# A hybrid decoder layer: three weight pieces issued earlier, and gate products split into single-pass matmuls

## The chip, the cores and the metric

The kernel runs on one core of a Trainium2 chip. The metric is the device time of one execution in microseconds (us). Before the change the median of three runs is 1207.89 us (1207.12 to 1209.24).

## The reference, cut to what matters

One layer over 256 prompt tokens and 8 x 8 sample tokens (320 in all), model width 1024. The change touches only the dense stage ahead of the mixture of experts:

```
proj = x @ w_in + b_in                       # 1024 -> 7 x 1024
xa, ga, b_gate, c_gate, v_sc, m_a, m_b = split(proj, 7)
xa_c = causal_dwconv(xa, width 4) + conv_a_b
r = sigmoid(blockdiag(wa) @ xa_c + ba)       # 16 heads of 64 x 64
i = sigmoid(blockdiag(wx) @ xa_c + bx)
a = exp(-8 r softplus(-lambda)); b = sqrt(1 - a^2) * i * xa_c
h = scan(a, b);  y_a = h * gelu(ga)
y_b = b_gate * causal_dwconv(c_gate * v_sc, width 3)
mixed = (sigmoid(m_a) * y_a + sigmoid(m_b) * y_b) @ w_out
```

Behind it stand a layer norm, a router, 32 experts of which each token takes 4, and a second layer norm. All inputs and outputs are float32.

## The kernel before, in words

The dense stage holds everything with channels on partitions. It runs in eight rounds c = 0..7, one for each group of 128 channels. A round takes seven pieces of `w_in`, each 1024 x 128, in the order XA, CG, V, GA, BG, MA, MB (j = 0..6); piece q = 7c + j is 512 KB.

A float32 product is made of three single-pass products in the type float32r. Each piece lands in one of four slots of `raw` (`load_piece`, L308 to L312). ScalarE rounds it to `w_hi` (L453, `split_high`); VectorE subtracts to get `w_lo` (L992, `split_low`, called `ahead(j)` in the rounds). TensorE then runs 8 x 3 matmuls over 320 tokens (L658): hi by hi, hi by lo, lo by hi. A piece may be loaded only when the split of the piece four before it is done (semaphore `lo_ok`), and TensorE starts a piece only when its own split is.

After the seventh piece of a round, TensorE multiplies the convolved `xc` by the two gate matrices of this round (L668). These are plain float32 matmuls, each recorded as two passes. The matrices are copied beforehand from `wab`, where all gate weights lie as 128 x 128 blocks, to `wcur` (L1064). TensorE waits for `wcur_ok`, `xc_ok` and for the banks of the gates to be free.

ScalarE takes each piece's result out of PSUM (L488 to L498), then the gate results through tanh (L502, L504), a second tanh (L507) and a square root (L509); only then does it reach the next `split_high`.

VectorE's order in a round is written out by hand: copy of the gate weights, `ahead(4)`, the first convolution (L1070 to L1077), `ahead(5)`, the second convolution (L1084 to L1092), `ahead(6)` to `ahead(9)`, in rounds 1 to 3 a `bias_low` for the expert biases (L1043), the merge of the gates MA and MB (from L1098), the wait for ScalarE's tanh, `ahead(10)`, a reciprocal (L1112), the scan (L1121) and the block of `mixT` (L1125).

SyncE issues nearly all loads in one queue, in program order: x, pieces 0 and 1, parameter rows, states, pieces 2 and 3, four loads of gate weights into `wab` (L352, 256 B rows; they need the memset of `wab`), eight loads of bias rows (L358, L360), then pieces 4 to 55, between which eight halves of the first experts' weights are issued (L331), one of them after `bias_ok`. At the end come the four loads of `w_out` (L378), the last of which waits for the last piece's products. VectorE waits for all gate weights once, ahead of round 0 (L1045).

After the rounds TensorE multiplies `mixT` by `w_out` (L678). The expert stage streams 192 units of 2 MB through ten slots; each load waits until TensorE has used the slot.

Of the kernel before, what the change touches and what calls it, by code (L numbers as in the profile page):

```python
# [13 lines left out]
P = 128  # L14
D = 1024
# [3 lines left out]
T = SEQ + NS  # L19
TILES = [(0, P), (P, P), (2 * P, NS)]  # L20
IN_W = 7 * D
NP = 7 * KC
# [16 lines left out]
XA, GA, BG, CG, V, MA, MB = range(7)  # L39
# [5 lines left out]
ALU = mybir.AluOpType  # L45
ACT = mybir.ActivationFunctionType
AX_X = mybir.AxisListType.X
F32 = mybir.dt.float32
F32R = mybir.dt.float32r
I32 = mybir.dt.int32  # L50
U32 = mybir.dt.uint32
ds = bass.ds
# [25 lines left out]
def hybrid_layer(nc, x_prompt, x_sample, state_h, state_conv, state_sc, w_in, b_in, conv_a_w,  # L78
# [5 lines left out]
    with ctx:  # L84
# [3 lines left out]
        def sem(name):  # L88
            return ctx.enter_context(nc.semaphore(name))
# [5 lines left out]
        slot = 4 * WIDE  # L95
        XT, X1 = SLOTS * slot, SLOTS * slot + 12 * D
# [4 lines left out]
        def place(name, shape, offset, dt=F32):  # L101
            return nc.alloc_sbuf_tensor_at(name, shape, dt, offset=base + offset)
# [36 lines left out]
        y_acc = x_tok  # L139
        wab = x1[:, 0:2, :].rearrange("p a (c n) -> p a c n", c=KC)  # L140
        st_rows = x1[:, 2, :]

# [34 lines left out]
        PS = ctx.enter_context(nc.psum_tensor("PS", [P, 8, HALF], F32))  # L179


        tiles = place("tiles", [P, 12 * T + 2 * P], 5 * slot)
        bgt, cgt, vt, gel, tma, tmb, xc, tr, ti, rr, aa, sq = (tiles[:, i * T:(i + 1) * T] for i in range(12))
        wcur = tiles[:, 12 * T:12 * T + 2 * P].rearrange("p (a n) -> p a n", a=2)
        hh = vt
        uc = cgt
        xa_p, xa_s = xa_pad[:, 0:259], xa_pad[:, 259:347].rearrange("p (b s) -> p b s", b=DB)
# [63 lines left out]
        gates_done, gates_taken = sem("gates_done"), sem("gates_taken")  # L251
        wcur_ok = sem("wcur_ok")
        prm_ok = sem("prm_ok")
        xa_free, cv_free, xc_ok, block_ok = sem("xa_free"), sem("cv_free"), sem("xc_ok"), sem("block_ok")
        t_ok, sq_ok = sem("t_ok"), sem("sq_ok")
        xlo_ok = sem("xlo_ok")
        wout_done, shifted = sem("wout_done"), sem("shifted")
# [49 lines left out]
        def _(sp):  # L307
# [36 lines left out]
            sp.dma_start(st_rows[0:8, :], state_h[0]).then_inc(st_in, 16)  # L344
            sp.dma_start(st_rows[8:32, :], state_conv[0].rearrange("b j d -> (b j) d")).then_inc(st_in, 16)
            sp.dma_start(st_rows[32:48, :], state_sc[0].rearrange("b j d -> (b j) d")).then_inc(st_in, 16)
            for q in range(2, 4):
                load_piece(q)
            sp.wait_ge(zero_ok, 1)
            for a, w in enumerate((lru_wa, lru_wx)):  # L350
                for j in range(2):
                    sp.dma_start(wab[64 * j:64 * j + 64, a, :, 64 * j:64 * j + 64],  # L352
                                 w[0].rearrange("(c j) i o -> j i c o", j=2)[j]).then_inc(wab_in, 16)

            for a in range(2):
                for h in range(2):
                    rows = slice(64 * a + 32 * h, 64 * a + 32 * h + NE)
                    sp.dma_start(bias_raw[rows, 0:2 * HALF].rearrange("p (b n) -> p b n", b=2),  # L358
                                 b_gu[0].rearrange("e (b a n) -> a e b n", a=2, b=2)[a]).then_inc(bias_in, 16)
                    sp.dma_start(bias_raw[rows, 2 * HALF:3 * HALF],  # L360
                                 b_down[0, :, a * HALF:(a + 1) * HALF]).then_inc(bias_in, 16)

            for q in range(4, NP):
                load_piece(q)
                if q % 4 == 3 and q < 7 + 4 * KC:
                    k = (q - 7) // 4
                    if k == 6:
                        sp.wait_ge(bias_ok, 1)
                    load_half(k // 2, k % 2)
# [49 lines left out]
            for q, (t, _) in enumerate(LAST_SUMS):  # L419
                t0, n = TILES[t]  # L420
# [26 lines left out]
        def _(act):  # L447
# [24 lines left out]
            for q in range(NP):  # L472
                c, j = q // 7, q % 7
                m = ORDER[j]
                bias = prm[:, BIN + m * KC + c:BIN + m * KC + c + 1]
                if 0 < q < NP - AHEAD:
                    split_high(q + AHEAD)
                if q == 5:
                    act.wait_ge(prm_ok, 3)
                if q == 8:  # L480
                    act.wait_ge(bias_in, 128)
                    act.activation(bias4[:, :, :].rearrange("p b n -> p (b n)"), bias_raw, ACT.Copy)\
                       .then_inc(bias_hi, 1)
                act.wait_ge(proj_done, q + 1)
                ps = PS[:, j % 6, 0:T]
                if m == XA:
                    act.wait_ge(xa_free, c + 1)
                    act.activation(xa_p[:, 3:259], pr(ps), ACT.Identity, bias=bias)  # L488
                    act.activation(xa_s[:, :, 3:11], sm(ps), ACT.Identity, bias=bias).then_inc(proj_taken, 1)
                elif m in (CG, V, BG):  # L490
                    if m == CG:
                        act.wait_ge(block_ok, c + 1)
                    act.activation({CG: cgt, V: vt, BG: bgt}[m], ps, ACT.Identity, bias=bias).then_inc(proj_taken, 1)
                elif m == GA:
                    act.activation(gel, ps, ACT.Gelu_apprx_tanh, bias=bias).then_inc(proj_taken, 1)
                else:
                    dst, o = (tma, c) if m == MA else (tmb, KC + c)
                    act.activation(dst, ps, ACT.Tanh, bias=bhalf[:, o:o + 1], scale=0.5).then_inc(proj_taken, 1)  # L498
                if j == 6:

                    act.wait_ge(gates_done, 2 * c + 2)
                    act.activation(ti, PS[:, 7, 0:T], ACT.Tanh, bias=ghalf[:, KC + c:KC + c + 1], scale=0.5)\  # L502
                       .then_inc(gates_taken, 1)
                    act.activation(tr, PS[:, 6, 0:T], ACT.Tanh, bias=ghalf[:, c:c + 1], scale=0.5)\  # L504
                       .then_inc(gates_taken, 1)
                    act.wait_ge(gates_taken, 2 * c + 4)
                    act.activation(tr, tr, ACT.Tanh, bias=sp2[:, c:c + 1], scale=sp2[:, c:c + 1]).then_inc(t_ok, 1)  # L507
                    act.wait_ge(t_ok, c + 1)
                    act.activation(sq, tr, ACT.Sqrt).then_inc(sq_ok, 1)  # L509
# [14 lines left out]
            for q, t in enumerate(T_ORDER):  # L524
                n = TILES[t][1]
# [76 lines left out]
            for q, (t, _) in enumerate(LAST_SUMS):  # L602
                n = TILES[t][1]
# [11 lines left out]
        def _(pe):  # L615
            mm = pe.matmul
# [15 lines left out]
            for k in range(KC):  # L632
                for t, (t0, n) in enumerate(TILES):
                    last = pe.transpose(PS[:, k, t0:t0 + n], x_tok[0:n, t, k * P:(k + 1) * P], ident[0:n, 0:n])
# [14 lines left out]
            for q in range(NP):  # L649
                c, j = q // 7, q % 7  # L650
                pe.wait_ge(lo_ok, q + 1)
                if q > 0:
                    pe.wait_ge(proj_taken, 7 * c + {0: 8, 6: 9}.get(j, j + 2))
                for k in range(KC):
                    if q == 0:
                        pe.wait_ge(xlo_ok, k + 1)
                    for n, (w, x) in enumerate(((w_hi, x_hi), (w_hi, x_lo), (w_lo, x_hi))):
                        last = mm(PS[:, j % 6, 0:T], w[:, q % RING, k, :], x[:, k, :],  # L658
                                  start=(k == 0 and n == 0), stop=(k == KC - 1 and n == 2))
                last.then_inc(proj_done, 1)  # L660
                if q == 0:
                    turn_rows()
                if j == 6:
                    pe.wait_ge(wcur_ok, c + 1)
                    pe.wait_ge(xc_ok, c + 1)
                    pe.wait_ge(gates_taken, 2 * c + 2)
                    for a in range(2):
                        mm(PS[:, 6 + a, 0:T], wcur[:, a, :], xc, start=True, stop=True).then_inc(gates_done, 1)  # L668

# [17 lines left out]
            for a in range(2):  # L689
                last = project(2, a, [KC - 1])  # L690
# [37 lines left out]
            for k in range(KC):  # L728
                last = pe.transpose(PS[0:54, 6 + k // 4, (k % 4) * P:(k % 4 + 1) * P], so[:, k, :], ident[:, :])
# [11 lines left out]
               start=False, stop=False)  # L741
# [241 lines left out]
        def _(dve):  # L983
# [53 lines left out]
            def bias_low(c, a):  # L1037

                if c == 1:
                    dve.wait_ge(bias_hi, 1)  # L1040
                rows = slice(64 * a + 32, 64 * a + 64)
                part = bias4[rows, c - 1, :]
                return dve.tensor_tensor(part, bias_raw[rows, (c - 1) * HALF:c * HALF], part.bitcast(F32), ALU.subtract)  # L1043

            dve.wait_ge(wab_in, 64)  # L1045
            for c in range(KC):
                def ahead(j):
                    if 7 * c + j < NP:
                        split_low(7 * c + j)

                def taken(j):
                    dve.wait_ge(proj_taken, c * 7 + (KC + j))
# [7 lines left out]
                def by_seq(ap, j):  # L1060
                    return ap.rearrange("p (b j) -> p b j", j=j)


                dve.tensor_copy(wcur[:, :, :], wab[:, :, ds(c, 1), :].rearrange("p a c n -> p (a c) n"))\  # L1064
                   .then_inc(wcur_ok, 1)

                link(dve.tensor_copy(xa_s[:, :, 0:3], by_seq(state(8, 24), 3)))
                ahead(4)
                taken(1)
                dve.tensor_scalar(pr(xc), xa_p[:, 0:SEQ], par(CAW, c), par(CAB, c), ALU.mult, ALU.add)  # L1070
                link(dve.tensor_scalar(sm(xc), xa_s[:, :, 0:DS], par(CAW, c), par(CAB, c), ALU.mult, ALU.add))
# [23 lines left out]
                    ahead(j)  # L1095
                if 1 <= c <= 3:
                    bias_low(c, 0)
                taken(7)  # L1098
                link(stt(tmb, tmb, 1.0, bgt, ALU.add, ALU.mult))
                link(dve.tensor_tensor(tmb, tmb, uc, ALU.mult))  # L1100
# [311 lines left out]
```

## Time and profile before

| | |
|---|---|
| profiled execution | 1207.79 us, span 1206.0 us |
| median of three runs | 1207.89 us |
| TensorE matmul busy | 1152.4 us (96%) |
| VectorE busy | 514.4 us (43%) |
| ScalarE busy | 255.7 us (21%) |
| mean granted TensorE clock | 0.992 |
| dense stage, to the end of the seventh piece of round 7 | 0 to 224.1 us |

Times in the rows count from the first instruction. PE is TensorE, PEld its weight loads, DVE VectorE, ACT ScalarE, SPq the queue of SyncE that issues DMAs. In a list in order of time a row gives start, duration, engine and line, operation, output and input, count, and in brackets the idle time of the engine ahead of it and what ended that. Neighbouring instructions of one line are merged (x24). Matmuls overlap, so their pace is read from the distance of their starts.

### The profile page before, as it was taken

The page shows a single profiled execution, that of the slowest core. Times are in us where ns is not written, and L with a number is a line of the kernel's source. Part 1 is how long each engine was busy: PE and PEld are TensorE (multiplying, and loading weights), DVE is VectorE, ACT ScalarE, POOL GpSimd, SP SyncE. Part 2 cuts the span into 40 slices and gives each one's busy share as a digit, 9 for nine tenths or more (in the row PEclk, how much of TensorE's full clock was granted, in tenths as well). Part 3 has the DMA queues.
Part 4 walks back from the last instruction along what each step waited for, and adds up shares of the span by engine and source line. Part 5 has one row for each costly group of instructions (what it writes and reads, how often), then busy time and mean ns, then how long its engine had stood idle before and what let it go on. Part 6 is the DMA issues. An engine that isn't in the chain of part 4 may idle for free.

```text
span 1206.0 us, 13920 instructions
## 1 busy us (share of the span) xinstructions
PE 1152.4 (96%) x5682; PEld 556.0 (46%) x5682; DVE 514.4 (43%) x982; ACT 255.7 (21%) x398; POOL 3.3 (0%) x13
## 2 busy tenths in 40 slices
PE   8999999999999999999999989999999999999994
PEld 8999999654333333333333323333333333333331
DVE  5888888563422322233323322232222222222236
ACT  4655655311111111111111111111111111111112
POOL 1000000000000000000000000000000000000000
PEclk9999999999999999999999999999999999999998
DMA  9766844748999999999999999999999999999994
GB/s 234 227 210 195 244 131 138 300 177 332 400 429 427 427 429 427 427 427 429 426 427 429 427 427 428 428 427 426 429 427 428 428 426 429 428 426 428 427 425 165
DMA packets 93404, 443.77 MB, mean 368 GB/s; under 512 B 7848, under 2 KB 65336, under 8 KB 67998
## 3 DMA queue, kind: packets, MB, share of 16 engines
q1 hardware_dynamic: 93246, 442.67, 90.7%
q8 instruction: 45, 0.74, 0.3%
q10 hardware_dynamic: 96, 0.22, 0.0%
q14 instruction: 17, 0.14, 0.0%
HBM read 441.34 MB, written 1.53 MB: 367 GB/s over the span
## 4 chain that ended last, share of the span: by engine, by line
PE 58%; DMA 28%; DVE 7%; issue 2%; ACT 2%; SPq 2%; DVEq 0%; ACTq 0%
DMA ring<-in_w_gu 24%; PE PS L846 20%; PE PS L886 13%; PE PS L658 7%; PE PS L754 6%; DMA ring<-in_w_down 3%; PE PS L776 3%; PE PS L678 2%; DVE w_lo L992 2%; DVE tiles L1035 1%; PE PS L762 1%; PE PS L769 1%; DVE tiles L1112 1%; PE PS L926 1%; PE PS L809 1%
## 5 line engine op out<-in xcount | busy, mean ns | idle before, releaser
L846 PE MATMUL PS<-ring,mid 128*64 128x512 f32 x1920 | 423.0, 594 | 24.4 <-DMA ring<-in_w_gu 23.7
L846 PEld LDWEIGHTS PS<-ring,mid 128*64 128x64 f32 x1920 | 135.4, 137 | 305.1 <-issue 254.8
L886 PE MATMUL PS<-ring,mid 128*64 128x512 f32 x960 | 213.1, 595 | 0.0
L1301 DVE TENSOR_SCALAR PS<-PS 128x512 f32<-128x512 f32 x30 | 21.0, 700 | 358.1 <-PE PS L846 358.1
L658 PE MATMUL PS<-x_hi,w_hi 128*128 128x320 f32 x448 | 141.5, 316 | 2.6 <-DVE w_lo L992 2.0
L658 PE MATMUL PS<-x_hi,w_lo 128*128 128x320 f32 x448 | 139.1, 311 | 0.0
L658 PE MATMUL PS<-x_lo,w_hi 128*128 128x320 f32 x448 | 139.1, 310 | 0.0
L1283 DVE TENSOR_TENSOR ys<-PS,ys 64x512 fp32r<-64x512 f32 x64 | 44.1, 688 | 193.9 <-ACT ys L572 185.6
L886 PEld LDWEIGHTS PS<-ring,mid 128*64 128x64 f32 x960 | 66.1, 137 | 130.1 <-issue 130.0
L1035 DVE SCALAR_TENSOR_TENSOR x_tok<-PS,gate,x_tok 128x1024 f32<-128x1024 f32 (+1 forms) x93 | 115.1, 1275 | 20.8 <-PE PS L776 20.8
L563 ACT ACTIVATE mid<-PS 128x512 f32<-128x512 f32 x30 | 17.9, 598 | 423.8 <-DVE PS L1301 423.8
L754 PE MATMUL PS<-x,onehot 128*64 128x512 f32 (+1 forms) x396 | 98.8, 617 | 2.9 <-DVE esel L1200 2.9
L658 PEld LDWEIGHTS PS<-x_hi,w_hi 128*128 128x128 f32 x448 | 84.7, 189 | 5.6 <-DVE w_lo L992 4.7
L658 PEld LDWEIGHTS PS<-x_lo,w_hi 128*128 128x128 f32 x448 | 84.7, 189 | 0.3
L658 PEld LDWEIGHTS PS<-x_hi,w_lo 128*128 128x128 f32 x448 | 84.7, 189 | 0.0
L572 ACT ACTIVATE ys<-PS 64x512 fp32r<-64x512 f32 x60 | 35.6, 593 | 209.1 <-PE PS L886 208.4
L992 DVE TENSOR_TENSOR w_lo<-raw,w_hi 128x1024 fp32r<-128x1024 f32 x56 | 67.0, 1223 | 19.9 <-ACT w_hi L453 19.4
L776 PE MATMUL PS<-ys,onehotT 128*128 128x512 f32 (+1 forms) x186 | 64.7, 431 | 0.0
L453 ACT ACTIVATE w_hi<-raw 128x1024 fp32r<-128x1024 f32 x56 | 59.1, 1055 | 21.2 <-DMA raw<-in_w_in 21.2
L754 PEld LDWEIGHTS PS<-x,onehot 128*64 128x64 f32 (+1 forms) x396 | 22.8, 136 | 55.9 <-issue 52.1
L776 PEld LDWEIGHTS PS<-ys,onehotT 128*128 128x128 f32 (+1 forms) x186 | 25.5, 176 | 25.4 <-issue 25.2
L678 PE MATMUL PS<-ring,mixT 128*128 128x512 f32 (+1 forms) x96 | 35.3, 597 | 1.4 <-DMA ring<-in_w_out 1.4
(232 smaller groups left out, 726.3 us busy)
## 6 DMA issues: line engine op xcount, KB each, us to landing
ring<-in_w_gu SPq DMA_DIRECT2D x124, 2048.0 KB, 39.8
ring<-in_w_down SPq DMA_DIRECT2D x62, 2048.0 KB, 38.8
raw<-in_w_in SPq DMA_DIRECT2D x56, 512.0 KB, 5.5
ring<-in_w_gu SPq DMA_DIRECT2D x8, 1024.0 KB, 8.2
ring<-in_w_out SPq DMA_DIRECT2D x4, 1024.0 KB, 6.0
ring<-in_w_down SPq DMA_DIRECT2D x4, 1024.0 KB, 41.4
x_tok<-in_x_prompt SPq DMA_DIRECT2D x1, 1024.0 KB, 5.4
out<-x SPq DMA_DIRECT2D x2, 512.0 KB, 2.7
```

What stands on the lines that cost most here:

```text
L453: act.activation(w_hi[:, q % RING], raw[:, q % RING], ACT.Copy).then_inc(hi_ok, 1)
L572: act.activation(y_rows(a, 0), PS[64 * a:64 * a + 64, XB, :], ACT.Copy).then_inc(yhi_ok, 1)
L658: last = mm(PS[:, j % 6, 0:T], w[:, q % RING, k, :], x[:, k, :], start=(k == 0 and n == 0), stop=(k == KC - 1 and n == 2))
L678: last = mm(out, mixT[:, k, t0:t0 + n], slot_out[:, k // 2, k % 2, a * HALF:(a + 1) * HALF], start=(k == 0), stop=(k == KC - 1))
L754: last = mm(PS[64 * a:64 * a + 64, XB, :], onehot[0:n, t, :], x1[0:n, t, a * HALF:(a + 1) * HALF], start=(t == 0), stop=(t == 2))
L776: last = mm(PS[0:n, bank + a, :], onehotT[:, par, t0:t0 + n], ys[:, a, :], start=True, stop=True)
L846: last = mm(PS[64 * a:64 * a + 64, b, :], xgT[:, 2 * (u % 2) + j, u // 2, :], w[:, o:o + HALF], start=False, stop=(u == 3 and j == 1))
L886: last = mm(PS[64 * a:64 * a + 64, XB, :], hT[:, j, u, :], w[:, j * D + a * HALF:j * D + (a + 1) * HALF], start=(u == 0 and j == 0), stop= ...
L992: dve.tensor_tensor(w_lo[:, q % RING], raw[:, q % RING], w_hi[:, q % RING].bitcast(F32), ALU.subtract).then_inc(lo_ok, 1)
L1035: return dve.scalar_tensor_tensor(out=out, in0=in0, scalar=scalar, in1=in1, op0=op0, op1=op1)
L1283: last = dve.tensor_tensor(y_rows(a, 1), PS[64 * a:64 * a + 64, bank, :], y_rows(a, 0).bitcast(F32), ALU.subtract)
L1301: dve.tensor_scalar(gm, gm, LIMIT, None, ALU.min).then_inc(gm_ok, 1)
```

## The change

On the loads: piece 4 is issued right behind pieces 2 and 3, ahead of the gate weights; pieces 5 and 6 are issued between the gate weights and the bias rows; the rest follows from piece 7.

On the gate products: ScalarE rounds `xc` to `xc_hi` after it has taken the BG piece; VectorE copies the gate weights to `gate_hi` (in place of the copy to `wcur`), subtracts to get `gate_lo` after `ahead(4)`, and subtracts to get `xc_lo` after `ahead(9)` and `bias_low`. TensorE runs three single-pass matmuls for each gate and waits for `xc_lo` (semaphore `xclo_ok`) in place of `xc_ok`. The new tiles lie in the space of the state rows, which have been read by then.

```
@@ sync
-            for q in range(2, 4):
+            for q in range(2, 5):
                 load_piece(q)
             sp.wait_ge(zero_ok, 1)
...
+            for q in range(5, 7):
+                load_piece(q)
             for a in range(2):
                 for h in range(2):
...
-            for q in range(4, NP):
+            for q in range(7, NP):
@@ scalar
                     act.activation({CG: cgt, V: vt, BG: bgt}[m], ps, ACT.Identity, bias=bias).then_inc(proj_taken, 1)
+                    if m == BG:
+                        act.wait_ge(xc_ok, c + 1)
+                        act.activation(xc_hi[:, :], xc, ACT.Copy).then_inc(xchi_ok, 1)
@@ tensor
                     pe.wait_ge(wcur_ok, c + 1)
-                    pe.wait_ge(xc_ok, c + 1)
+                    pe.wait_ge(xclo_ok, c + 1)
                     pe.wait_ge(gates_taken, 2 * c + 2)
                     for a in range(2):
-                        mm(PS[:, 6 + a, 0:T], wcur[:, a, :], xc, start=True, stop=True).then_inc(gates_done, 1)
+                        for n, (w, x) in enumerate(((gate_hi, xc_hi), (gate_lo, xc_hi), (gate_hi, xc_lo))):
+                            last = mm(PS[:, 6 + a, 0:T], w[:, a, :], x[:, :], start=(n == 0), stop=(n == 2))
+                        last.then_inc(gates_done, 1)
@@ vector
-                dve.tensor_copy(wcur[:, :, :], wab[:, :, ds(c, 1), :].rearrange("p a c n -> p (a c) n"))\
-                   .then_inc(wcur_ok, 1)
-
+                gates_w = wab[:, :, ds(c, 1), :].rearrange("p a c n -> p (a c) n")
+                dve.tensor_copy(gate_hi[:, :, :], gates_w)
                 link(dve.tensor_copy(xa_s[:, :, 0:3], by_seq(state(8, 24), 3)))
                 ahead(4)
+                dve.tensor_tensor(gate_lo[:, :, :], gates_w, gate_hi[:, :, :].bitcast(F32), ALU.subtract)\
+                   .then_inc(wcur_ok, 1)
                 taken(1)
...
                 if 1 <= c <= 3:
                     bias_low(c, 0)
+                dve.wait_ge(xchi_ok, c + 1)
+                dve.tensor_tensor(xc_lo[:, :], xc, xc_hi[:, :].bitcast(F32), ALU.subtract).then_inc(xclo_ok, 1)
                 taken(7)
```

## Rows read from the trace of the kernel before

**Rows 1.** Chain of waits in order of time: start, duration, engine and line.
```profile
63.96 3.79 PE PS L658 x24
...
220.30 3.80 PE PS L658 x24
...
224.12 7.58 DMA ring<-in_w_out
```
**Rows 2.** Weight loads' waits, 0 to 260 us: total, times, longest.
```profile
PEld PS L658 <- DVE w_lo L992: 4.7, 8, 2.3
```
**Rows 3.** TensorE in order of time, round 0.
```profile
26.95 0.31 PE L658 MATMUL PS<-x_hi,w_lo 128*128 128x320 f32 x1
29.30 0.42 PE L658 MATMUL PS<-x_hi,w_hi 128*128 128x320 f32 x1 [2.04 <-DVE w_lo L992]
...
30.39 0.47 PE L658 MATMUL PS<-x_hi,w_hi 128*128 128x320 f32 x1
30.66 0.47 PE L658 MATMUL PS<-x_lo,w_hi 128*128 128x320 f32 x1
...
41.35 0.31 PE L658 MATMUL PS<-x_hi,w_lo 128*128 128x320 f32 x1
```
**Rows 4.** TensorE in order of time, end of round 5, and at w_out.
```profile
168.12 0.41 PE L658 MATMUL PS<-x_hi,w_hi 128*128 128x320 f32 x1
...
171.59 0.31 PE L658 MATMUL PS<-x_hi,w_lo 128*128 128x320 f32 x1
171.73 1.24 PE L668 MATMUL PS<-tiles 128*128 128x320 f32 x4
...
231.83 4.71 PE L678 MATMUL PS<-ring,mixT 128*64 128x512 f32 x12 [1.36 <-DMA ring<-in_w_out]
```
**Rows 5.** SyncE's queue in order of time.
```profile
11.14 2.72 SPq L352 DMA_DIRECT2D x<-in_lru_wa  x2
...
21.92 1.05 SPq L312 DMA_DIRECT2D raw<-in_w_in  x2
```
**Rows 6.** Line 352 alone: time from issue to landing of its loads.
```profile
DMA to landing us min/median/max: 5.1/6.2/6.9
```
**Rows 7.** ScalarE in order of time.
```profile
26.86 1.06 ACT L453 ACTIVATE w_hi<-raw 128x1024 fp32r<-128x1024 f32 x1 [7.71 <-DMA raw<-in_w_in]
...
168.05 0.53 ACT L498 ACTIVATE tiles<-PS,dsm 128x320 f32<-128x320 f32 x1 [2.04 <-PE PS L658]
```
**Rows 8.** VectorE in order of time, start and round 0.
```profile
10.62 1.22 DVE L992 TENSOR_TENSOR w_lo<-raw,w_hi 128x1024 fp32r<-128x1024 f32 x1 [0.45 <-ACT w_hi L453]
...
22.70 0.28 DVE L1064 COPY tiles<-x 128x256 f32<-128x256 f32 x1
...
28.02 1.23 DVE L992 TENSOR_TENSOR w_lo<-raw,w_hi 128x1024 fp32r<-128x1024 f32 x1 [4.95 <-ACT w_hi L453]
...
32.08 1.22 DVE L992 TENSOR_TENSOR w_lo<-raw,w_hi 128x1024 fp32r<-128x1024 f32 x1
...
36.09 3.50 DVE L992 TENSOR_TENSOR w_lo<-raw,w_hi 128x1024 fp32r<-128x1024 f32 x3
```
**Rows 9.** VectorE in order of time, rounds 2, 4 and 5.
```profile
93.38 0.68 DVE L1043 TENSOR_TENSOR bias<-bias_raw,bias 32x512 fp32r<-32x512 f32 x1
...
144.49 1.23 DVE L992 TENSOR_TENSOR w_lo<-raw,w_hi 128x1024 fp32r<-128x1024 f32 x1 [0.20 <-ACT w_hi L453]
...
163.98 0.42 DVE L1084 TENSOR_TENSOR dsm<-tiles 128x256 f32<-128x256 f32 x1
164.31 0.23 DVE L1085 TENSOR_TENSOR dsm<-tiles 128x64 f32<-128x64 f32 x1
...
166.84 4.63 DVE L992 TENSOR_TENSOR w_lo<-raw,w_hi 128x1024 fp32r<-128x1024 f32 x4
```
**Rows 10.** Stretches: busy us and count by engine, granted clock, DMA share, GB/s.
```profile
30.00:32.00 2.00, 2.00 (x11) 2.00 (x10) 1.93 (x8) 1.72 (x3) 0.00 (x0) 0.53 1.10 385
...
224.00:262.00 38.00, 36.64 (x105) 14.84 (x104) 21.76 (x44) 4.89 (x9) 0.00 (x0) 1.00 0.59 242
```

More of the change, by code:

```diff
@@ L141, in hybrid_layer @@
         st_rows = x1[:, 2, :]
+        xc_hi = place("xc_hi", [P, T], X1 + 8 * D, F32R)
+        xc_lo = place("xc_lo", [P, T], X1 + 8 * D + 4 * T, F32R)
+        gate_lo = place("gate_lo", [P, 2, P], X1 + 8 * D + 8 * T, F32R)
         x_hi = place("x_hi", [P, KC, T], 6 * slot, F32R)
@@ L179, in hybrid_layer @@
         PS = ctx.enter_context(nc.psum_tensor("PS", [P, 8, HALF], F32))
-        tiles = place("tiles", [P, 12 * T + 2 * P], 5 * slot)
+        tiles = place("tiles", [P, 12 * T], 5 * slot)
         bgt, cgt, vt, gel, tma, tmb, xc, tr, ti, rr, aa, sq = (tiles[:, i * T:(i + 1) * T] for i in range(12))
-        wcur = tiles[:, 12 * T:12 * T + 2 * P].rearrange("p (a n) -> p a n", a=2)
+        gate_hi = place("gate_hi", [P, 2, P], 5 * slot + 48 * T, F32R)
         hh = vt
@@ L254, in hybrid_layer @@
         xa_free, cv_free, xc_ok, block_ok = sem("xa_free"), sem("cv_free"), sem("xc_ok"), sem("block_ok")
+        xchi_ok, xclo_ok = sem("xchi_ok"), sem("xclo_ok")
         t_ok, sq_ok = sem("t_ok"), sem("sq_ok")
```

## The prediction

> **What bounds the kernel now.** Read the chain of waits in order of time first, then what TensorE waited for, then the single instructions around the places the chain names. The dense stage is eight rounds c = 0..7 of seven projection pieces (piece 7c + j, j = 0..6, 24 matmuls each); call S(c) the start of the seventh piece (j = 6) of round c. In the chain [rows 1] the reader is to see three things. The seventh piece of every round from 1 to 7 stands in it as a step of its own (first 63.96, last 220.30, seven of them, some 26.05 us apart). It is entered from the VectorE split `w_lo`: TensorE's weight loads waited eight times for L992, 4.7 us in all, 2.3 of it once [rows 2], so about 0.35 us in each of the seven other rounds. And the stage ends through the last w_out load, issued when the last piece is done (224.12, landing 7.58 us later), not through the last gate products. So a round is a loop: seventh piece, gate products (L668), ScalarE (tanh, square root), VectorE (reciprocal, scan, next convolution), split of the next seventh piece. VectorE closes it and TensorE has only a third of a microsecond to spare. Everything behind hangs on S(7), because the first expert loads are gated by the last piece, the last block, the projection and x1: I carry a shift of S(7) one to one to the end.
>
> The first wait is another thing. Piece 4 is issued at 21.92 [rows 5], behind four loads of gate weights and eight of bias rows; its high part starts at 26.86 after ScalarE stood 7.71 us [rows 7]; TensorE stops after 26.95 and starts again at 29.30 [rows 3]. Then the stream runs at a start every 0.267 us (30.39 to 30.66) and not 0.147 (171.59 to 171.73 in [rows 4]), with a granted clock of 0.53 in 30 to 32 us [rows 10], the 1.2 GHz level for nearly all of that stretch. S(0) is 41.35 - 23 x 0.147 = 37.97.
>
> **Part 1, the loads.** Piece 4 needs the split of piece 0, done at 10.62 + 1.22 = 11.84 [rows 8], so SP issues it at about 11.9 instead of 21.92; pieces 5 and 6 need splits 1 and 2, done at the latest when TensorE starts piece 2 (27.10 - 48 x 0.147 = 20.0), and follow the gate weights: SP spent 21.92 - 11.14 = 10.8 us on twelve loads [rows 5], so it is at piece 5 some 4 to 5 us after 12.4. At the 4.9 us that piece 4 took (21.92 to 26.86), or half as much again, all three land before their use. The gate weights move from 11.14 to about 12.4, 1.3 us later, and have 0.5 MB more ahead of them. They took 5.1 to 6.9 us to land [rows 6], the last issued near 15. VectorE comes to them at 22.70 [rows 8]; the last of them now lands at about 22 to 23.7, so VectorE stands up to 1 us. Is that hidden? From there it needs, by its old spacing, 0.4 us to split 4, then 32.08 - 28.02 = 4.06 plus a new subtraction of 0.33 to split 5, and 36.09 - 32.08 = 4.01 to split 6, plus 1.22 [rows 8]: 10.0 us. TensorE, with no stop, comes to piece 6 at 26.95 + 0.147 + 48 x 0.147 = 34.15. So the weights may land as late as 24.1 at no cost. I take S(0) = 34.15: **-3.8 us** (2.2 of stop, 1.6 of slow stream). Bias rows and pieces 7 to 9 come 2.6 us later or earlier against the round but are used only from S(0) + 1 on; if piece 9 lands late it costs up to 0.5. Ends: -3.8 and -2.5.
>
> **Part 2, VectorE's two subtractions.** `gate_hi` replaces a copy of the same 128x256 (0.28, [rows 8]): nothing. `gate_lo` is one more 128x256 subtraction of two SBUF tensors, between the split j = 4 and the convolution, where VectorE is on the chain in all rounds. The nearest row is L1084, 128x256 of two tensors: next instruction 164.31 - 163.98 = 0.33 later, itself 0.42 long [rows 9]. Below: 0.20, as a copy; above: 0.42. I take 0.33. It lies in the seven intervals S(c) to S(c+1): **+2.3 us**.
>
> `xc_lo` (128x320; rows of that size take 0.49, as L1043 with 512 elements takes 0.68 [rows 9] and L1084 with 256 takes 0.42) stands behind the splits j = 6..9, and now the gate products wait for it. Queued behind them on TensorE is all of the next round. VectorE's order decides:
> Rounds 5 and 6: four splits from 166.84, spaced (4.63 - 1.22)/3 = 1.137 [rows 9], so `xc_lo` runs 171.39 to 171.88 and TensorE sees it at 171.93 (0.05 as from split to piece: 166.84 + 1.22 to 168.12). Before, the products began at 171.73 [rows 4].
> Rounds 1 to 3: `bias_low` stands between, 93.38 [rows 9] + 0.68 - 0.09 overlap, so `xc_lo` ends at 94.46, seen 94.51, which is S + 4.51; before S + 3.61.
> Round 4: its last split starts only at 144.49 [rows 9]: seen at 146.17, S + 4.14.
> Round 0: the split of piece 9 ends near S + 2.8, `xc_lo` before S + 3.5: no wait. Round 7 has no splits left and is off the path.
>
> **Part 3, the products.** Four passes, 171.73 to + 1.24 [rows 4], end at S + 4.85. Six single passes at 0.147: unhindered they end at 3.61 + 5 x 0.147 + 0.31 = S + 4.65, **-0.20** (round 0). After a wait the first is 0.41 long [rows 4], so they end 0.41 + 0.735 = 1.15 after it: rounds 5 and 6 S + 4.96, **+0.11 each**; rounds 1 to 3 S + 5.66, some **+0.83 each** (round 1's bias row starts a tenth later); round 4 S + 5.29, **+0.43**. ScalarE's next step waits for both products, so these are the loop's. Bounds of a pass: 0.147 and 0.267. The other new instruction, ScalarE's `xc_hi` (about 0.5), comes ahead of a 2.04 us idle [rows 7] and its split is needed 2 us later: nothing; uncovered it would be 0.5 a round.
>
> **Sum.** -3.8 + 2.3 - 0.2 + 3 x 0.83 + 0.43 + 2 x 0.11 = +1.4 us. Against the profiled execution, 1207.79 (span 1206.0), that is 1209.2; the median of the runs, 1207.89, stands 0.1 above it: **1209.3 us**. TensorE loses the gain of the start again in three rounds.
>
> Two rules weighed. The row says that a VectorE instruction starts 0.08 before the one ahead of it ends (1.22 long, 1.137 apart, [rows 9]). The Trainium skill, "VectorE: DVE Perf Modes", section "Terms", says of the flush after every operation: "next op can't issue until 8-slice pipe empties". By that the two subtractions would cost about 0.09 more each in seven rounds, +1.3 us; the trace disagrees for the splits, so it is only rival 3. On the loads: the gate weights landed in 5.1 to 6.9 us for 128 KB each [rows 6], against 4.9 for a 512 KB piece [rows 5, 7]. The Trainium skill, "DMA: Bandwidth & Descriptors", section "Specifications", asks for at least 512 B per transfer for line rate, and these move rows of 64 floats, 256 B. It speaks against putting anything ahead of them; by the row the cost is the 1 us of standing counted above, hidden.
>
> **Rivals.**
> 1. TensorE is the bound and VectorE follows. For it: it is 96% busy over the span, and waits only 0.35 us a round [rows 2]. Then only the start counts and the products give 0.2 in seven rounds: -5.2, 1202.6. Half of it, the wait for `xc_lo` costing nothing but `gate_lo` counting: -3.8 - 1.4 + 2.3 = -2.9, 1205.0. Against: the wait for the split recurs in all seven rounds, so VectorE is late already.
> 2. The clock falls again in the new stops. Place: ahead of the products in rounds 1 to 3, about 1 us each. Price: the 1.6 us paid after the stop of 2.2, three times: +4.8, 1214.1, slower. It decides if such a stop is enough. Against: a stop of 1.36 at 231.83 left the granted clock at 1.00 [rows 4, 10].
> 3. VectorE's added work costs full lengths: +2.7, 1210.6, slower by a little more than can be told.
> 4. The start gives less: gate weights land after 24.1, each microsecond later costs one, or piece 4 waits for an instruction ahead of it in ScalarE's or VectorE's order, so that the reordering does not do what it says: 2 us lost, 1211.3.
>
> **How the numbers follow.** Forecast 0.52, rival 1 0.15, rival 2 0.08, rival 3 0.15, rival 4 0.10. A measurement of this kernel can tell about 0.2%, 2.4 us, from no change: 1205.5 to 1210.3. Of the forecast's share 0.42 lies within, 0.07 above, 0.03 below; rival 1 is faster; rivals 3 and 4 are half within and half above; rival 2 above. Faster 0.18, same 0.54, slower 0.28. The likeliest case alone spans 1207.5 to 1211 (its bounds: `gate_lo` 0.20 to 0.42, the start -2.5); the range takes in half of rival 1 and most of rival 4: 1205 to 1212.5.
>
> **What would show it.** After: no stop of TensorE near 27 us and no 0.267 spacing at 30 (part 1); S(0) near 34.1; VectorE's copy of the gate weights at 22.7 to 23.7. Intervals S(c) to S(c+1) of 26.1 in round 0, 27.2 in 1 to 3, 26.8 in 4, 26.5 in 5 and 6. The products start on a wait for VectorE's subtraction, 1 us in rounds 1 to 3, 0.2 in 5 and 6; the waits for `w_lo` at the seventh piece stay and grow to 0.5. S(7) near 221.7. The prediction is wrong if intervals stay at 26.05 or less, if the seventh piece no longer waits, or if the granted clock dips in rounds 1 to 3.

## The result, and the profile after

The changed kernel is slower: median 1214.12 us (1212.82 to 1217.17, four runs) against 1207.51 (1206.55 to 1209.24, four runs), a ratio of 1.0062 on record (95% interval 1.0048 to 1.0076; the two medians alone give 1.0055, and the ratios below are likewise those on record). The forecast was 1209.3, at most 1212.5. The profiled execution is the longest of the four (1217.17, span 1214.3; the shortest span is 1211.0), so of the rows below those behind the dense stage show its upper end.

Chain of waits after, in order of time (start, duration, engine and line; L667 are the projection matmuls, L678 the gate products, L689 the product with w_out). It answers to [rows 1] and [rows 3].

```profile
16.54 21.32 PE PS L667 x144
37.86 2.63 issue
40.48 1.78 PE PS L678 x6
42.26 25.51 PE PS L667 x168
...
91.09 3.78 PE PS L667 x24
94.88 0.89 issue
95.76 1.13 PE PS L678 x6
...
225.29 3.80 PE PS L667 x24
...
229.11 8.83 DMA ring<-in_w_out
...
238.07 31.60 PE PS L689 x72
```

The stop near 27 us is gone: 144 projection matmuls run without a gap to 37.86, so S(0), reckoned from the start of the last matmul (37.55, below) as in the prediction, is 37.55 - 23 x 0.147 = 34.17 (forecast 34.15, before 37.97). Then comes a step that the chain before did not have: 2.63 us of "issue" ahead of the first gate products. "Issue" hides its releaser here; TensorE's own rows show the place, and what the stop did to the stream behind it (the bracket is the idle time before a row):

```profile
37.55 0.31 PE L667 MATMUL PS<-x_hi,w_lo 128*128 128x320 f32 x1
40.48 0.44 PE L678 MATMUL PS<-xc_hi,gate_hi 128*128 128x320 f32 x1 [2.63 <-issue]
40.73 0.47 PE L678 MATMUL PS<-xc_hi,gate_lo 128*128 128x320 f32 x1
...
44.15 0.31 PE L667 MATMUL PS<-x_hi,w_lo 128*128 128x320 f32 x1
```

Starts are 0.25 to 0.27 us apart up to 43.9 and 0.147 from 44.15. Busy time by stretch (columns as in [rows 10], the granted clock third from the end) gives the clock beside it:

```profile
40.00:42.00 2.00, 1.51 (x6) 1.55 (x7) 1.77 (x4) 0.00 (x0) 0.00 (x0) 0.67 1.03 395
42.00:44.00 2.00, 2.00 (x9) 2.00 (x9) 0.00 (x0) 1.65 (x4) 0.00 (x0) 0.50 1.03 324
...
94.00:120.00 26.00, 24.89 (x167) 24.25 (x167) 22.54 (x51) 15.26 (x22) 0.00 (x0) 1.00 0.61 174
238.00:240.00 2.00, 1.93 (x5) 0.73 (x6) 0.38 (x1) 0.00 (x0) 0.00 (x0) 0.66 0.94 389
```

The 1.2 GHz stretch has moved from 30 us [rows 10] to 42 us; it has not gone. It does not come in round 2 (94 to 120), where the stop is 0.89. It comes again at 238, behind a stop of 2.81 us for w_out that was 1.36 before [rows 4].

Why do the products wait at 37.86? VectorE's rows, then ScalarE's, then SP's queue:

```profile
22.43 0.29 DVE L1076 CAST gate_hi<-x 128x256 fp32r<-128x256 f32 x1
...
37.02 1.22 DVE L1003 TENSOR_TENSOR w_lo<-raw,w_hi 128x1024 fp32r<-128x1024 f32 x1 [3.13 <-ACT w_hi L459]
...
38.76 1.22 DVE L1003 TENSOR_TENSOR w_lo<-raw,w_hi 128x1024 fp32r<-128x1024 f32 x1 [0.51 <-ACT w_hi L459]
...
39.90 0.48 DVE L1111 TENSOR_TENSOR xc_lo<-tiles,xc_hi 128x320 fp32r<-128x320 f32 x1
```
```profile
31.57 1.06 ACT L459 ACTIVATE w_hi<-raw 128x1024 fp32r<-128x1024 f32 x1 [1.89 <-DMA raw<-in_w_in]
...
35.93 1.06 ACT L459 ACTIVATE w_hi<-raw 128x1024 fp32r<-128x1024 f32 x1 [2.52 <-DMA raw<-in_w_in]
...
37.67 1.06 ACT L459 ACTIVATE w_hi<-raw 128x1024 fp32r<-128x1024 f32 x1 [0.27 <-DMA raw<-in_w_in]
```
```profile
20.39 1.88 SPq L364 DMA_DIRECT2D bias_raw<-in_b_gu  x1
...
27.02 0.42 SPq L316 DMA_DIRECT2D raw<-in_w_in  x1
27.49 0.58 SPq L335 DMA_DIRECT2D ring<-in_w_gu  x1
28.11 7.67 SPq L316 DMA_DIRECT2D raw<-in_w_in  x4
```

Read from the bottom: SP spends 20.39 to 27.0 on the eight bias rows, issues piece 7 at 27.02, then a 1 MB half unit of the expert weights, then pieces 8 and 9. Their high parts wait for the DMA three times, by 1.89, 2.52 and 0.27 us, and the splits on VectorE follow at 32.67, 37.02 and 38.76. `xc_lo` stands behind all of them in VectorE's program and is done at 40.38, 0.10 before TensorE goes on. Before, the gate products read the convolution's output directly, and nothing in them waited for a split.

### The profile page after: what moved, and what is told of

Read it like the earlier page. It is cut to its first block, busy times and chain, and to the rows that moved or that the text cites. A ratio compares the mean times of both kernels' runs of the same rounds, so it can differ in the third digit from the quotient of the medians.

```text
span 1214.3 us, 13976 instructions
## 1 busy us (share of the span) xinstructions
PE 1156.5 (95%) x5698; PEld 558.5 (46%) x5698; DVE 520.3 (43%) x998; ACT 257.6 (21%) x406; POOL 3.3 (0%) x13
## 4 chain that ended last, share of the span: by engine, by line
PE 62%; DMA 25%; DVE 9%; issue 2%; ACT 2%; DVEq 0%; POOL 0%; ACTq 0%; POOLq 0%
PE PS L857 22%; DMA ring<-in_w_gu 21%; PE PS L897 14%; PE PS L765 6%; PE PS L667 6%; DMA ring<-in_w_down 3%; PE PS L787 3%; PE PS L689 3%; DVE w_lo L1003 2%; DVE tiles L1046 2%; PE PS L773 1%; DVE tiles L1126 1%; PE PS L780 1%; PE PS L820 1%; PE PS L937 1%
## 5 line engine op out<-in xcount | busy, mean ns | idle before, releaser
L857 PE MATMUL PS<-ring,mid 128*64 128x512 f32 x1920 | 423.2, 594 | 23.0 <-DMA ring<-in_w_gu 22.7
L667 PE MATMUL PS<-x_hi,w_hi 128*128 128x320 f32 x448 | 140.6, 314 | 1.3 <-DVE w_lo L1003 1.3
L667 PE MATMUL PS<-x_lo,w_hi 128*128 128x320 f32 x448 | 139.0, 310 | 0.0
L667 PE MATMUL PS<-x_hi,w_lo 128*128 128x320 f32 x448 | 138.9, 310 | 0.0
L667 PEld LDWEIGHTS PS<-x_hi,w_hi 128*128 128x128 f32 x448 | 84.6, 189 | 4.1 <-DVE w_lo L1003 3.9
L667 PEld LDWEIGHTS PS<-x_lo,w_hi 128*128 128x128 f32 x448 | 84.6, 189 | 0.0
L667 PEld LDWEIGHTS PS<-x_hi,w_lo 128*128 128x128 f32 x448 | 84.5, 189 | 0.0
L689 PE MATMUL PS<-ring,mixT 128*128 128x512 f32 (+1 forms) x96 | 37.0, 619 | 2.8 <-DMA ring<-in_w_out 2.8
```

Source lines behind the costliest of these rows:

```text
L689: last = mm(out, mixT[:, k, t0:t0 + n], slot_out[:, k // 2, k % 2, a * HALF:(a + 1) * HALF], start=(k == 0), stop=(k == KC - 1))
L857: last = mm(PS[64 * a:64 * a + 64, b, :], xgT[:, 2 * (u % 2) + j, u // 2, :], w[:, o:o + HALF], start=False, stop=(u == 3 and j == 1))
```

## The experiments

Each kernel was timed in five rounds beside the kernel before on the same chip. e1 to e12 are their short names. First the two parts by themselves.

**The loads alone** (e1), on the kernel before:

```diff
-            for q in range(2, 4):
+            for q in range(2, 5):
                 load_piece(q)
...
+            for q in range(5, 7):
+                load_piece(q)
...
-            for q in range(4, NP):
+            for q in range(7, NP):
```

> The new order of loads with the gate products as before. Theory A (the loads' gain of 3.8 us is real and is thrown away only because the gate products now wait behind the splits of pieces 8 and 9, whose loads land late): the gate products of round 0 start at S(0) + 3.6, near 37.7, the seventh piece of round 1 near 60.2, and all of the 3.8 us stay: 1203.8. Theory B (the late pieces 8 and 9 hold round 0 whatever the gate products wait for, through VectorE's order): S(1) near 63.5 and 1207, within 0.5 of before.

1203.77 against 1206.39: ratio 0.9980 (0.9971 to 0.9988), 2.6 us faster, and S(7) at 217.74, 2.6 earlier. The loads do what the prediction said, for less: S(0) is 34.73, and S(1) 61.54, 2.4 earlier than before. The same late pieces 7 to 9 are in this trace (waits of 1.34, 2.89 and 0.23 us), but the products do not depend on splits; the lateness only makes ScalarE late to free a bank of PSUM (the memory that holds the matmuls' results), for which the first piece of round 1 waits:

```profile
40.35 0.38 PE L660 MATMUL PS<-x_hi,w_hi 128*128 128x320 f32 x1 [0.87 <-ACT tiles L500]
```

**The split products alone** (e2): the changed kernel with SP's order of before (the diff above, reversed).

> The split gate products with the old order of loads. Theory A: round 0 costs +0.1, rounds 1 to 6 together +4.8 as in the changed kernel (27.2 us a round in 1 to 3, 26.5 in 4 to 6), and what follows the w_out load 0 to 3 us: 1212.7 to 1215, as slow as the whole change. Theory B (the loads are what makes the change slow, by the stop of 2.9 us ahead of the first gate products and the fallen clock behind it): 1209 or less.

1214.56: ratio 1.0058 (1.0045 to 1.0071), as slow as the whole change. S(0) is 36.92 and S(7) 224.83, so seven rounds take 187.9 instead of 182.3 [rows 1, 3], +5.6, where parts 2 and 3 together forecast +5.2. The 0.4 is round 0: its products do not stop, but they start at S(0) + 3.85, where the forecast had S(0) + 3.61. So the split is sized about right, and the 2.6 us that the loads give alone are worth nothing under it.

This profile shows one thing more. It has the kernel before's order of loads, and its first stop is 1.10 us and not 2.04, with the granted clock at 1.00 from 26 to 38 us. e11 below, whose dense stage is the kernel before's, has 0.83 there, the clock at 1.00, and S(0) at 36.59 and S(7) at 218.90. So the 2.04 us and the slow stream behind it are those of one profiled execution; how often they come is not known. Against e11 the moved loads bring S(0) forward by 2.4, not 3.8.

**Who holds the products up in round 0?** On the changed kernel, the half units two pieces later (e4); then that and the eight bias rows behind piece 9 as well (e5):

```diff
-            for a in range(2):            # the bias rows' loop
...
             for q in range(7, NP):
                 load_piece(q)
+                if q == 9:
+                    for a in range(2):    # the bias rows' loop, e5 alone
...
-                if q % 4 == 3 and q < 7 + 4 * KC:
-                    k = (q - 7) // 4
+                if q % 4 == 1 and 9 <= q < 9 + 4 * KC:
+                    k = (q - 9) // 4
```

> The whole change, with each half of an expert unit issued two pieces later, so that the first stands behind piece 9 and not between pieces 7 and 8. Theory A1 (that 1 MB load ahead of piece 8 makes pieces 8 and 9 late): they land 3 us earlier, the stop ahead of round 0's gate products goes from 2.9 us to under 0.5, the clock doesn't fall there, S(1) near 60.4: 3.8 us less than the change, 1210.3. Rival A2 (the bias rows ahead of piece 7 do it): the stop stays over 2 us and the time within 1 us of the change, 1214.

1211.35, ratio 1.0040 (1.0027 to 1.0053). The stop shrank by 1 us only: piece 7 is still behind the bias rows, issued at 27.84, and its high part begins at 33.54. (The changed kernel's own stop differs between profiles: it is 2.63 in the profile above, 1.92 in e8 and 2.75 in e9, whose dense stage is the same.)

```profile
37.97 1.62 issue
39.59 1.13 PE PS L678 x6
...
62.26 3.78 PE PS L667 x24
```

> The whole change, with the bias rows issued behind piece 9 (they stood ahead of piece 7) and each half unit two pieces later. e4 left a stop of 1.6 us, as piece 7 was still late and held ScalarE's splits. Theory A (the failed step of the prediction is only the late pieces 7 to 9): pieces 7 to 9 are split in time, the stop ahead of round 0's products is under 0.4 us, S(1) near 60.4, the other intervals stay at 27.2 and 26.5, S(7) near 221.7, 1.4 us behind the kernel before; with the unsteady part behind the w_out load +1.4 to +3.5. Rival A3 (something else in round 0 holds the products, ScalarE's order or the parameters): the stop stays over 1.3 us and the time 5 us above before.

1209.78, ratio 1.0028 (1.0019 to 1.0036): 2.8 us over the kernel before, with the split in it. The stop is gone and S(1) is where the prediction had it (60.25):

```profile
37.82 0.95 PE PS L678 x6
...
60.43 3.78 PE PS L667 x24
...
118.75 1.75 issue
...
222.66 3.79 PE PS L667 x24
...
226.47 6.29 DMA ring<-in_w_out
```

S(7) is 222.66 (forecast 221.7). The missing 0.9 is the stop at 118.75, 1.75 where rounds 1 and 2 have 0.89. ScalarE and VectorE ahead of it, one row each:

```profile
116.87 1.06 ACT L459 ACTIVATE w_hi<-raw 128x1024 fp32r<-128x1024 f32 x1 [1.55 <-DMA raw<-in_w_in]
```
```profile
117.96 1.23 DVE L1003 TENSOR_TENSOR w_lo<-raw,w_hi 128x1024 fp32r<-128x1024 f32 x1 [0.78 <-ACT w_hi L459]
```

The last split waited for its high part, and that for its piece. A half unit is issued 4 us ahead of that piece (106.95 and 110.95). e4 has the same half unit there; the piece's high part waits 0.68 in it, and the stop stays at 0.88. So the order of the loads makes this piece late in both, but what made it later in e5 is not shown.

**The wait for `xc_lo` and `gate_lo`.** On the changed kernel both subtractions are moved up, right behind the split of the seventh piece (j = 6) and ahead of the three splits j = 7 to 9, where they wait for ScalarE's `xc_hi` (e3); and `xc_lo` alone (e7):

```diff
-                dve.tensor_tensor(gate_lo[:, :, :], gates_w, gate_hi[:, :, :].bitcast(F32), ALU.subtract)...
...
+                    if j == 6:
+                        dve.wait_ge(xchi_ok, c + 1)
+                        dve.tensor_tensor(xc_lo[:, :], xc, xc_hi[:, :].bitcast(F32), ALU.subtract)...
+                        dve.tensor_tensor(gate_lo[:, :, :], gates_w, gate_hi[:, :, :].bitcast(F32), ALU.subtract)...
...
-                dve.wait_ge(xchi_ok, c + 1)
-                dve.tensor_tensor(xc_lo[:, :], xc, xc_hi[:, :].bitcast(F32), ALU.subtract)...
```

> The whole change, with both of VectorE's subtractions right behind the split of the seventh piece (ahead of splits j = 7 to 9) instead of ahead of the convolution and behind the splits. Theory A (they cost by their place: gate_lo lies on VectorE's way to the seventh piece, xc_lo on the gate products' way): no stop ahead of the products in any round, intervals of 25.85 us, S(7) 5.2 earlier than before: 1202.4. Rival C (VectorE's time is what counts, wherever it is spent): intervals stay at 26.5 and above, 1207 or more.

1204.71, ratio 0.9985 (0.9976 to 0.9994). VectorE no longer closes the rounds; TensorE runs through them at 25.7 to 25.9 us a round:

```profile
39.72 24.87 PE PS L667 x168
64.59 0.88 PE PS L678 x6
...
91.29 24.93 PE PS L667 x168
116.22 0.88 PE PS L678 x6
...
215.90 3.80 PE PS L667 x24
```

The 6 products take 0.88 in the chain, the 4 of the kernel before took 1.09 there: 0.2 a round is all that the split gives, once nothing waits. It shows rival 1's case, TensorE the bound, as one that this placement makes and the changed kernel's did not.

> The whole change with only the xc_lo subtraction moved ahead of the splits j = 7 to 9; gate_lo stays ahead of the convolution. If gate_lo costs its 0.33 us on VectorE's way to the seventh piece, the intervals are 26.05 - 0.20 + 0.33 = 26.2 us in all rounds, against 25.8 to 25.9 in e3: S(7) 2.0 later than e3, near 218, and xc_lo's place is then worth the rest, 7 us, of which 2.9 are round 0's stop and the clock behind it. If gate_lo is hidden, the intervals are those of e3.

1206.60, ratio 1.0004 (0.9993 to 1.0014); S(7) 217.79, rounds of 26.10 to 26.22. With `gate_lo` on VectorE's chain VectorE closes the rounds again. The 26.05 of before, less 0.2 for the products, plus the 0.33 of part 2 makes 26.18 (an estimate): `gate_lo` costs what was forecast, and S(7) is 1.9 later than in e3.

**The late loads and both placements mended** (e6: e5's loads, e3's placement):

> As e5, and both subtractions behind the split of the seventh piece as in e3. Theory A: no stop anywhere in the dense stage, TensorE bound by its own 25.8 us a round; against e3 the 1.0 us that TensorE stood ahead of round 1 (for ScalarE, which was held by pieces 8 and 9) goes too: S(7) near 214.9, 5.4 us before the kernel before, time 3.3 to 5.4 us less. Rival: no better than e3, whose time was 0.15% below before.

1202.24, ratio 0.9967 (0.9953 to 0.9980): 4.7 us under its kernel before of 1206.95, the lowest ratio of the study, though its interval still touches e3's. S(1) is 60.64, S(7) 215.70, and the last w_out load lands in 6.17 us. Expected was 214.9 for S(7): once the subtractions are moved, the later bias rows and half units bring it only 0.2 forward against e3.

**The clock in round 0's stop.** On the changed kernel, ten matmuls whose results are overwritten, ahead of the wait, in round 0 alone (e12):

```diff
                     pe.wait_ge(wcur_ok, c + 1)
-                    pe.wait_ge(xclo_ok, c + 1)
                     pe.wait_ge(gates_taken, 2 * c + 2)
+                    if c == 0:
+                        for _ in range(10):
+                            mm(PS[:, 6, 0:T], x_hi[:, 0, 0:P], x_hi[:, 0, :], start=True, stop=True)
+                    pe.wait_ge(xclo_ok, c + 1)
```

> The changed kernel with ten more 128x320 matmuls on TensorE in round 0 alone, whose results are overwritten, between the last projection piece of the round and its wait for xc_lo. Theory C: of the 4.0 us by which S(1) came later than forecast (64.25 against 60.25), 2.6 are the stop before the gate products and about 1.4 the clock that falls in it (products 1.78 instead of 1.13 us, the 168 matmuls behind 25.51 instead of 24.7). The filler takes 1.5 us of the stop, which shrinks to about 1.2 with the products starting where they did (near 40.5); the granted clock stays at 1.00, the 168 matmuls take 24.7 and S(1) comes near 62.9. Round 1 is then closed by TensorE; S(7) near 223.9 and the time 1.4 below the changed kernel, near 1212.6. Rival V: the stop alone makes the loss, since VectorE's split closes the round whatever TensorE's clock does: S(1) stays within 0.3 of 64.25 and the time at 1214.

1213.70 against 1207.49, ratio 1.0054 (1.0041 to 1.0068). TensorE's rows, the chain and the stretches in this kernel (L681 are its products):

```profile
37.44 1.63 PE L677 MATMUL PS<-x_hi 128*128 128x320 f32 x10
41.04 0.42 PE L681 MATMUL PS<-xc_hi,gate_hi 128*128 128x320 f32 x1 [1.97 <-DVE xc_lo L1114]
```
```profile
41.04 1.16 PE PS L681 x6
...
225.49 3.80 PE PS L667 x24
```
```profile
42.00:44.00 2.00, 2.00 (x16) 2.00 (x15) 0.49 (x2) 1.73 (x4) 0.00 (x0) 1.00 0.98 347
```

Here TensorE's wait has its name: `xc_lo`. The clock stays at 1.00, the full 2.4 GHz level. The products start 0.56 later (piece 9 came 0.6 later in this execution) and take 1.16 instead of 1.78, so they end at 42.20 against 42.26, and S(7) is 225.49 against 225.29: nothing gained. Both theories had a part wrong. S(1) came 0.35 earlier (63.74 against 64.09; the 64.25 of the expectation is a quarter of a microsecond too late), but round 1 gave it back. The end of the products sets the round: from it to the next seventh piece's start lie 21.5 us on ScalarE and VectorE (42.20 to 63.74 here, 40.72 to 62.26 in e4). In the changed kernel it is 21.8, as TensorE comes 0.3 late, but from the end of these products to the start of round 1's lie 26.23 us there and 26.26 here: TensorE's slow stream up to 44.1 is hidden. What is left of the fallen clock is the 0.6 us by which it stretches the products themselves; that these would be gained in a run whose piece 9 is no later was not shown. Nor is the stream always hidden: in e8 the clock falls only behind the products (end 41.24), and round 1's products start 26.74 us later, 0.5 more.

**Behind S(7).** Two attempts on the stop before w_out. A filler of six matmuls there (e8):

```diff
                 pe.wait_ge(block_ok, k + 2)
+                if k == 6:
+                    pe.wait_ge(bias_ok, 1)
+                    keep_warm(6, 5)
                 pe.wait_ge(wout_in[k // 2], 16)
```

> The whole change, with six matmuls of 128x512 (1.3 us, results unused) ahead of the wait for the last w_out load. Theory D (the stop of 2.8 us there lets the clock fall, which costs 1.65 us in the w_out product, and whether it falls makes the runs of this kernel spread over 4 us): the granted clock stays at 1.00 behind the stop, the w_out product takes 29.95 us and not 31.6, the runs lose their upper half; median 1 to 1.5 us below the change, whose ratio to before was 1.0062. Rival: the clock has no part in it, the ratio stays at 1.0062 or more.

1213.99, ratio 1.0063 (1.0050 to 1.0076). In the profile the 72 matmuls take 29.95 and the clock does not fall there, as that theory wanted, but the median stays where the changed kernel's is. Its profiled execution was again an end of the spread (1212.59, the shortest of six), so it does not decide it.

Then the last w_out load by itself, the expert units behind it issued only when it has landed, on the changed kernel (e9), on e6's version (e10) and on the kernel before (e11):

```diff
             sp.wait_ge(proj_done, NP)
+            sp.wait_ge(wout_in[3], 16)
             load_unit(4)
```

> The changed kernel, with one wait added on SP: the first of the two 2 MB expert units that SP issues 0.4 to 1.0 us behind the last w_out load now waits until that load has landed. Theory T: what the changed kernel loses behind S(7) (3.3 us in its profile) is the last w_out load, which shares the DMA engines with these two units (8.83 us for 1 MB, against some 4 alone, an estimate from 6.2 us in the best profile), plus the clock that falls in the stop it makes. By it the load lands in about 4.5 us, TensorE does not stop there (stop 2.81 -> 0), the 72 w_out matmuls take 29.95 and the kernel ends at S(7) + 981 instead of S(7) + 984 to 989: S(7) 225.3, product ends about 261, span about 1207 and time 1209 (ratio 1.0015). Rival U: the later start of the expert units is paid behind, because from 300 us on the DMA engines are at 1.0 share: the time stays at 1213 or is 3 to 5 us above.

> The version of e6 (late bias rows and half units, both subtractions right behind the last high split) with the same added wait. There the load landed in 6.17 us and TensorE stopped 0.15. Theory T: 0.15 to gain, time 1202 (ratio 0.9965). Rival U: the units come 4 us later for nothing, time 1204 to 1206.

> The kernel before with the same added wait only. TensorE stopped 1.36 there for a load that took 7.58 us. Theory T: 1.4 faster (ratio 0.9988), product ends at 260.4. Rival U: same or 2 to 4 us slower.

1214.02 (ratio 1.0061), 1203.17 (0.9975) and 1206.52 (0.9999, 0.9990 to 1.0007), each against 1206.41. The expert units behind it are not what makes the load slow: with none issued before it has landed, it takes as long; the rows of e9, e10 and e11:

```profile
229.43 7.60 DMA ring<-in_w_out
```
```profile
219.24 7.44 DMA ring<-in_w_out
```
```profile
222.72 7.42 DMA ring<-in_w_out
```

But it was not alone on the DMA engines. SP's queue and two stretches of e9 (columns as in [rows 10]; DMA share and GB/s stand last):

```profile
225.58 0.89 SPq L384 DMA_DIRECT2D ring<-in_w_out  x2
```
```profile
229.00:231.00 2.00, 2.00 (x13) 1.35 (x13) 0.97 (x2) 1.21 (x3) 0.00 (x0) 1.00 1.02 418
235.00:237.00 2.00, 0.58 (x4) 0.00 (x0) 1.85 (x7) 0.00 (x0) 0.00 (x0) 1.00 0.09 31
```

The second and third w_out loads, 1 MB each, are issued together when the last piece is split, 3.9 us ahead of the fourth. The engines are busy with the three of them from 227.5 to 235, at about 400 GB/s, and for the last 2 us before the landing at 237.03 they move next to nothing. So a sharing of the engines is not refuted, only that with the expert units; issuing the second and third load earlier was not tried. The fourth landed after 6.2 to 8.9 us in the fourteen profiles of these kernels, and in e6's version it was faster with the units behind it (6.17) than without (7.44). What makes this difference is open.

## Why the prediction was wrong

**The step that failed** is the last sentence of part 1, "if piece 9 lands late it costs up to 0.5", and with it part 3's round 0, "no wait" (-0.20). I had put the split of piece 9 near S(0) + 2.8. It ended at S(0) + 5.8 (39.98 against 34.17). I had followed each load up to its use except those behind the moved ones: the high parts of pieces 7 to 9 began at 31.57, 35.93 and 37.67, only 1.6, 0.8 and 1.0 us earlier than in the kernel before (33.21, 36.69, 38.66), while the round that uses them had come 3.8 us forward, and the products had just been given a reason to wait for their splits.

The sizes close. Forecast end of round 0's products: 34.15 + 4.65 = 38.8. Measured 42.26: 3.46 later, of which 2.63 is the stop, 0.63 the fallen clock in the six products (1.78 against 1.15), and 0.1 the longer first pass behind a stop; the last 0.1 lies between 37.76, where the forecast has the products start, and 37.86, from where the stop counts. Added to the forecast S(7) of 221.7 that is 225.2; measured 225.29. Against the kernel before S(7) moved by +5.0 instead of +1.4.

**Part 1 otherwise** was right: no stop at 27, the gate weights' copy at 22.43 (forecast 22.7 to 23.7), S(0) within 0.02. e5 shows the whole gain arriving at S(1), 60.43 against 60.25. But the 3.8 us were read from one execution, and the first stop is not the same in others (2.04 us in it, 1.10 in e2, 0.83 in e11); one profile could not tell that.

**Parts 2 and 3 for rounds 1 to 6** were right. Intervals from S(1) = 64.09: 27.00, 27.27, 27.26, 26.63, 26.52, 26.52, forecast 27.2 three times, 26.8, 26.5 twice; their sum is 161.2, forecast 161.5. The 0.3 is round 1, where TensorE came late to its seventh piece while VectorE did not. The wait ahead of the products is 0.72, 0.89 and 0.88 in rounds 1 to 3. VectorE's order behind it, `bias_low` between the splits and `xc_lo`, reads as forecast [rows 9]:

```profile
62.54 4.63 DVE L1003 TENSOR_TENSOR w_lo<-raw,w_hi 128x1024 fp32r<-128x1024 f32 x4
67.20 0.68 DVE L1054 TENSOR_TENSOR bias<-bias_raw,bias 32x512 fp32r<-32x512 f32 x1
67.90 0.49 DVE L1111 TENSOR_TENSOR xc_lo<-tiles,xc_hi 128x320 fp32r<-128x320 f32 x1
```

**"I carry a shift of S(7) one to one to the end"** held only roughly. What does hold is the end of the 72 w_out matmuls: from there to the end of the span lie 944.1 to 945.1 us in the profiles of the kernel before, the changed one and e1 to e8 (before 231.83 + 29.95 = 261.78, span 1206.0; after 269.67, 1214.3); in e9 to e12 it is up to 946.4. Between S(7) and that end the profiles have 40.1 to 44.5 us: the landing of the last w_out load, and 1.65 us more where TensorE's stop for it made the clock fall (31.60 against 29.95). The profiled execution after has both (8.83 against 7.58, and the clock), 2.9 us. So its 9.4 us over the one before (1217.17 against 1207.79) are 5.0 to S(7), 2.9 behind it, 0.4 in the rest of the span and 1.1 around the span. For the medians, which differ by 6.6, the split is not known, since only one execution of each was profiled. S(7) itself is no fixed number: 224.66 (e8), 225.29, 225.49 (e12) and 225.61 (e9) for the dense stage of the changed kernel, and 220.30 and 218.90 (e11) for the one before, a shift of 4.4 to 6.7. That the runs of the changed kernel (spans 1211.0, 1211.1, 1213.5, 1214.3) differ by the tail behind S(7) is likely but was not shown, and why the w_out load takes longer in some executions is open.

**The rivals.** Rival 2 had the right mechanism and the wrong place: a clock fall in a new stop, not in rounds 1 to 3 (0.72 to 0.89 us long, clock 1.00) but in round 0 and at w_out. Its price for a stop also counted a slow stream that VectorE hides here. That its time, 1214.1, is also the measured one is luck: it added 1.6 us for each of three stops behind which the clock stayed at 1.00, and it did not have the 2.63 us of standing in round 0. Rival 4 had the loss at the start, but from pieces and gate weights ahead of S(0), which came in time. Rival 1 fell: the seventh piece still waits for `w_lo`, as TensorE's waits over 0 to 260 us show (total, times, longest; it answers to [rows 2]):

```profile
PEld PS L667 <- DVE w_lo L1003: 3.9, 11, 0.5
```

Rival 3, full lengths, would have made the rounds 26.27 in e7 and 26.7 in rounds 5 and 6 of the changed kernel; they are 26.10 to 26.22 and 26.52. The rule weighed with it (the Trainium skill, "VectorE: DVE Perf Modes", section "Terms") does not show here either.

One bound of the prediction does not follow from its terms: `gate_lo` at 0.20 takes 0.9 off, which makes 1208.4 and not 1207.5. Nothing hangs on it.

## What to carry to other kernels

When a change pulls a stage forward, list the loads *behind* the moved ones and give each a landing time against the new clock of the stage; the queue does not move forward with the work. When a new operand is made behind other work on an in-order engine, its price is whatever that work waits for, in the worst round and not only in the usual one: put it ahead of that work (from e5, where round 0 no longer stops, to e6 it is still 7.0 us of S(7)). When a term is read from one profile, look whether a second execution has it: the stop that the loads were to remove was 2.04 us in one and 0.83 in another. And look for the step at which a round is closed (here the end of the gate products), since slowness elsewhere in the round, even a halved clock, cost the changed kernel nothing (in e8 it was 0.5 us).

## What the runs showed of the hardware

In the dense stage and at w_out the clock fell to the 1.2 GHz level behind TensorE stops of 1.92 (e8, granted clock 0.50 in 42 to 44 us), 2.04 [rows 3], 2.63, 2.75 (e9), 2.81 and 2.87 us (e2's stop for w_out, 31.65 us behind it), and not behind 1.62 (e4), 1.75 (e5), 1.91 (e12, for w_out) nor 1.97 (e12, behind the filler). Stops of 1.9 to 2.0 went both ways, and each of these falls lasted some 3 us of work. The length of a stop does not decide alone: near 720 us every profile has one of 2.86 us in the expert stage, and behind it the granted clock was 0.50 in the kernel before (724 to 726 us), still 0.50 in 736 to 740 us in the changed one, where the stop ends at 730.92, and 1.00 throughout in e11 (720 to 734 us). The stream costs 0.147 us a matmul at the high level and 0.267 at the low one. The surprise was how little of that reached the end. And a 1 MB load behind two others needed 7.4 to 7.6 us to land with nothing issued behind it (e9 to e11), about the 7.58 of the kernel before, with 4 MB issued right behind it; in e9 the engines stood nearly idle (31 GB/s) for the last 2 us of that.
